# One program per engine, normalisations in pairs, gate stores from another queue, and prefetched rows in pieces in a two-stage encoder block

## The reference

```python
h = rms_norm(x, norm_mix); proj = h @ w_in           # q,k,v | B,C,u | two gates
att = stick_breaking_attention(q, k, v)              # 8 heads x 64, causal
y_a = att @ w_branch_a
y_b = (B * causal_conv3(C * u)) @ w_branch_b
x = x + (sigmoid(ga) * y_a + sigmoid(gb) * y_b) @ w_out
hx = rms_norm(x, norm_ffn)                           # second normalisation
q = (hx @ w_q).reshape(n, 8, 2, 128)
s = einsum('nhpc,hpkc->nhpk', q, sub_keys)           # 16 lists of 128 scores
# top 16 of each list, top 16 of the 16x16 sums -> 8*16 experts per token
w = softmax(best) * gelu(u_sel . hx)                 # u_sel, v_sel: rows of 16384x1024 tables
x = x + sum(w * v_sel)
out = rms_norm(x, final_norm)
```

## Time and profile before

| | |
|---|---|
| median of 3 runs | 1786.6 us (1784.12 to 1790.11) |
| the profiled execution's own time | 1788.63 us |
| its span, first to last instruction | 1786.9 us |
| PE busy | 1718.5 us, 96% of the span |
| first program | 0 to about 526 us |
| steps of the second program | about 526 to 1254 us |
| sums | 1254 to 1776 us |

### The profile page before, as it was taken

How to read it: one execution, slowest core, us unless ns; L and a number is a source line. 1 busy time by engine, 2 the same in 40 slices (tenths; PEclk the granted TensorE clock), 3 DMA queues, 4 the chain that set the end, 5 groups by cost and what they waited for, 6 DMA issues and landing times.

```text
span 1786.9 us, 24919 instructions
## 1 busy us (share of the span) xinstructions
PE 1718.5 (96%) x9066; PEld 1528.6 (86%) x9066; DVE 1278.5 (72%) x1834; ACT 768.5 (43%) x1086; POOL 775.1 (43%) x486
## 2 busy tenths in 40 slices
PE   6999999998979999999999999997999999999997
PEld 4777778877869999999999999997888888888886
DVE  1555511114889899989999797976678777877786
ACT  5444433234213466656666465553332332233222
POOL 3323334332411366655666678884333233323330
PEclk9999999998989999999999999998999999999999
DMA  4222223322225667766776899889999999999982
GB/s 153 71 71 68 62 71 94 105 71 71 83 83 204 204 239 245 243 234 240 244 244 224 317 341 345 289 309 340 345 395 350 351 364 347 349 358 358 347 328 104
DMA packets 211428, 413.79 MB, mean 232 GB/s; under 512 B 11408, under 2 KB 150704, under 8 KB 205744
## 3 DMA queue, kind: packets, MB, share of 16 engines
q1 hardware_dynamic: 154352, 228.63, 37.6%
q0 software_dynamic: 36864, 134.23, 20.8%
q10 hardware_dynamic: 20160, 50.34, 7.5%
HBM read 360.73 MB, written 52.43 MB: 231 GB/s over the span
## 4 chain that ended last, share of the span: by engine, by line
PE 51%; DVE 7%; POOL 7%; DMA 2%; ACT 2%; issue 2%; ACTq 0%; DVEq 0%; POOLq 0%
PE psum L1133 27%; PE psum L1073 19%; POOL ring L1274 4%; PE psum L1063 3%; POOL grid L1293 2%; DVE ring L1391 2%; DMA expert_gate<-grid 2%; DVE ul L1316 1%; PE psum L1100 1%; POOL hot L1284 1%; DMA ring<-in_expert_u,index 1%; DVE hot L1379 1%; DVE acc L1396 1%; DVE hot L1381 1%; ACT hot L1190 0%
## 5 line engine op out<-in xcount | busy, mean ns | idle before, releaser
L1073 PE MATMUL psum<-xTh,uh 128*128 128x384 f32 x1024 | 356.9, 349 | 17.5 <-DVE ul L1316 17.1
L1073 PE MATMUL psum<-xTl,uh 128*128 128x384 f32 x1024 | 346.0, 338 | 0.0
L1073 PE MATMUL psum<-xTh,ul 128*128 128x384 f32 x1024 | 345.8, 338 | 0.0
L1274 POOL DMA_INDIRECT ring<-in_expert_v,index x128 | 177.8, 1389 | 349.5 <-DVE acc L1396 307.2
L218 POOL TENSOR_TENSOR wl<-raw,wh 128x1024 fp32r<-128x1024 f32 x72 | 172.4, 2401 | 329.5 <-ACT wh L490 329.5
L1133 PE MATMUL psum<-vh,dwl 128*128 128x512 f32 x768 | 298.8, 389 | 0.0
L1133 PE MATMUL psum<-vl,dwh 128*128 128x512 f32 x768 | 298.8, 389 | 0.0
L1133 PE MATMUL psum<-vh,dwh 128*128 128x512 f32 x768 | 298.8, 389 | 0.0
L1210 ACT ACTIVATE vh<-v_raw 128x4096 fp32r<-128x4096 f32 x32 | 116.2, 3632 | 338.8 <-PE psum L1133 304.7
L1274 POOL DMA_INDIRECT ring<-in_expert_u,index x128 | 179.6, 1403 | 130.1 <-DVE index L1341 59.0
L1391 DVE SCALAR_TENSOR_TENSOR ring<-ring,x 128x1024 f32<-128x1024 f32 x128 | 206.4, 1625 | 26.3 <-DMA ring<-in_expert_u,index 24.9
(11 more groups left out here) (189 smaller groups left out, 2800.8 us busy)
## 6 DMA issues: line engine op xcount, KB each, us to landing
u_raw<-in_expert_u SPq DMA_DIRECT2D x128, 512.0 KB
v_raw<-in_expert_v SPq DMA_DIRECT2D x32, 2048.0 KB, 12.0
expert_act<-hb ACTq DMA_DIRECT2D x128, 192.0 KB
expert_gate<-grid ACTq DMA_DIRECT2D x12, 2048.0 KB
dh<-expert_act SPq DMA_DIRECT2D x32, 768.0 KB, 4.4
dg<-expert_gate SPq DMA_DIRECT2D x32, 768.0 KB
raw<-in_w_in SPq DMA_DIRECT2D x40, 512.0 KB, 3.8
raw<-in_w_q SPq DMA_DIRECT2D x16, 512.0 KB, 3.9
```

What stands on the lines that cost most here:

```text
L1073: last = nc.tensor.matmul(zb[s][:, 0:DT], w[s][:, c, :], x[:, c, 0:DT], start=(c == 0 and i == 0), stop=(c == C - 1 and i == 2))
L1274: nc.gpsimd.indirect_dma_start(out=ring[k][:], out_offset=None, in_=tables[x // SLOTS], in_offset=bass.IndirectOffsetOnAxis(ap=index[:, x ...
```

## The change

It does five things. (1) The two programs become functions for each engine, called one after the other inside one `nc.Block()`; the wait between them is gone, PE transposes the rows of step 0 before the last projection, and PSUM banks of the steps are swapped for that. ACT instead of DVE copies the score lists, and DVE does squares of the second normalisation; DVE leaves parts 4 to 11 of head 6 to the second program's steps 0 to 2 (9, 6 and 5 parts there, where 4, 4 and 4 stood). (2) The first normalisation's scales are made in pairs of blocks; scaled rows are written in column halves; each `norm_project` multiplies with `wh` first and with `wl` in a second pass. (3) The four small parameter loads are issued by ACT, and the weight loads start when the third block of x is there. (4) SP issues the twelve stores of `grid`, between its loads of buffers 1 and 2. (5) The first two groups of expert_v are loaded in eight pieces of 512 KB, one for each of the rounds 22 to 29, and the loads of `dh` no longer wait for the last store.

The diff, without indentation changes and cut to its core:

```diff
-    with nc.Block() as block:
-        @block.sync
-        def _(sp_):
+    def mix_sync(sp_):
...
-            sp_.wait_ge(S["rows_in"], 64)
+            sp_.wait_ge(S["consts"], 1)
+        sp_.wait_ge(x_in[2], 16)
...
+        def norm_project(first, r, parts):
+            ring = len(nb_ring)
+            for ready, more, blocks in parts[:-1]:
+                pe.wait_ge(S["xn_ready"], ready)
+                if more:
+                    pe.wait_ge(S["xn_more"], more)
+                for c in range(ring):
+                    norm_transposes(c, blocks)
+            pe.wait_ge(w_hi[0], r + 1)
+            pe.wait_ge(taken[0], r)
+            for c in range(C):
+                for n, x in enumerate((xh, xl)):
+                    pe.wait_ge(S[("xT_hi", "xT_lo")[n]], first + c + 1)
+                    nc.tensor.matmul(pj[0][:], wh[0][:, c, :], x[:, c, :], start=(c == 0 and n == 0), stop=False)
...
+                if c + ring < C:
+                    norm_transposes(c + ring, blocks)
+            pe.wait_ge(w_lo[0], r + 1 + PRIMED)
+            for c in range(C):
+                last = nc.tensor.matmul(pj[0][:], wl[0][:, c, :], xh[:, c, :], start=False, stop=(c == C - 1))
...
-            norm_project(0, NB, 0)
+        norm_project(0, 0, ((2, 0, (0, 1)), (3, 1, (2, 3)), (5, 1, range(NB))))
...
-            norm_project(C, 2 * NB, L5)
+        norm_project(C, L5, ((7, 3, range(NB)), (11, 3, range(NB))))
...
+        pe.wait_ge(u_in[0], 16)
+        for c in range(C):
+            last = nc.tensor.transpose(psum[6 + c // 4][:, c % 4 * P:c % 4 * P + P], u_raw[0][:, c * P:(c + 1) * P], ident[:])
+        last.then_inc(ut_full[0], 1)
             project(1, L5 + LISTS // 2 - 1, xh, xl)
...
             high(0, 0)
+        norm_hi(0, 0)
             high(1, 0)
             nc.scalar.preload_act_table_set("natural_log_exp_and_others")
-            norm_hi(0, 0)
...
+            norm_hi(C, C)
+        high(1, L4 + C // 2)
...
+        def copy_list(i, slot):
+            act.wait_ge(S["s_full"], i * 2 + (slot + 1 + PRIMED))
+            nc.scalar.activation(score[:, :, at, :], zt[slot][:].rearrange("p (b o k) -> p b o k", b=NB, o=1), ACT.Copy).then_inc(S["s_out"], 1)
...
+        for h in range(HEADS - 1):
+            dve.wait_ge(S["s_out"], h * 2 + 2 + PRIMED)
+            for k in range(12 if h < HEADS - 2 else AHEAD):      # AHEAD = 4
+                rank(dve, h, k)
...
+        def send(q):
+            sp_.wait_ge(S["g_sum"], 8 * q + 8 + PRIMED)
+            sp_.dma_start(gd[:, :, :].rearrange("b p x -> p b x")[:, q:q + 1, :], grid[:].rearrange("p j n -> p (j n)").unsqueeze(1)).then_inc(S["g_out"], 16)
...
+        for r in range(1, STEPS // 4):
+            load(r, range(2))
+            if 4 * r - 4 in SEND:
+                send(SEND[4 * r - 4])
+            load(r, range(2, 4))
+            if V_EARLY <= r < V_EARLY + 2 * G4:                  # V_EARLY = 22
+                if r == V_EARLY:
+                    sp_.wait_ge(S["selT_full"], DB)
+                load_part(*divmod(r - V_EARLY, G4))
+        for s in range(2):
+            load_acts(s, slice(s, s + 1))
...
             high(0)
+        last_list()
             for n in range(STEPS):
                 if n + 1 < STEPS:
                     high(n + 1)
-                if n in SEND:
-                    send(SEND[n])
...
                 if n < 3:
-                    for k in range(4 * n, 4 * n + 4):
-                        rank(dve, HEADS - 1, k)
+                if n == 0:
+                    dve.wait_ge(scores_out, LISTS + PRIMED)
+                for k in range((AHEAD, 13, 19)[n], (13, 19, 24)[n]):
+                    rank(dve, HEADS - 2 + k // 12, k % 12)
```

More of the change, by code:

```diff
@@ L47 @@
 PRIMED = 1
+AHEAD = 4
 Q0, K0, V0 = 0, SBW, 2 * SBW
@@ L514, in pair @@
-            def pair(p, r, before=None):
-                high(2, r)
-                take(0, r, qT[:], scale=HD ** -0.5)
+            act.wait_ge(S["var_ready"], g + 1)
+            nc.scalar.activation(rs[:, 2 * g:2 * g + 2], var[:, 2 * g:2 * g + 2], ACT.Sqrt).then_inc(S["root_ready"], 1)
+        act.wait_ge(S["scales"], 2)
+        nc.scalar.activation(xn[:, NB - 1, 0:T], acc[:, NB - 1, 0:T], ACT.Copy, scale=rs[:, NB - 1:NB]).then_inc(S["xn_more"], 1)
+        high(0, 0)
+        norm_hi(0, 0)
@@ L517, in pair, with gated @@
+        pair(0, 0)
+        with act.Fori(1, PAIRS) as p:
+            pair(p, p * 2, before=p - 1)
+        R0 = PAIRS * 2
+        def gated(r, c, before=None):
+            both_highs(c)
+            if before is not None:
                 high(0, r + 1)
-                take(1, r, kT[:])
+                exps(before, 0)
                 high(1, r + 1)
-                if before is not None:
-                    exps(before, 0)
-                    exps(before, 1)
-                take(2, r, vT[:])
@@ new lines, in mix_scalar @@
+        take_keys(2)
+        take_keys(3)
+        nc.scalar.preload_act_table_set("sqrt_and_others")
+        act.wait_ge(S["oT_full"], C - 2 + PRIMED)
+        take(0, L4 + C // 2 - 1, ot[0][:])
+        high(0, L4 + C // 2)
+        take(1, L4 + C // 2 - 1, ot[1][:])
+        act.wait_ge(S["x_added"], C + PRIMED)
+        for b in range(NB // 2, NB):
+            nc.scalar.activation(squared[:, b, D - 2 * P:D], acc[:, b, D - 2 * P:D], ACT.Square,
+                                 accum_out=ss[:, 1, b:b + 1]).then_inc(S["sq_done"], 1)
@@ new lines, in mix_scalar, with take_query @@
+        act.wait_ge(S["var_ready"], 3)
+        nc.scalar.activation(rs, var, ACT.Sqrt).then_inc(S["root_ready"], 1)
+        act.wait_ge(S["scales"], 3)
+        for b in range(NB // 2, NB):
+            nc.scalar.activation(xn[:, b, 0:T], acc[:, b, 0:T], ACT.Copy, scale=rs[:, b:b + 1]).then_inc(S["xn_more"], 1)
+        norm_hi(C, C)
+        high(1, L4 + C // 2)
+        def take_query(i, slot):
+            act.wait_ge(S["s_full"], i * 2 + PRIMED)
+            take(slot, i + (L4 + C // 2), ot[slot][:])
```

1839 lines of the change are left out of this document (923 added, 916 removed).

## The result

The changed kernel takes 1768.3 us in the median (1768.17 to 1768.36, 4 runs), the kernel before beside it 1785.4 us (1783.02 to 1790.11, 4 runs). The ratio is 0.9897, 95% interval 0.9883 to 0.9911: faster, by some 17 us or 1%. The profiled execution took 1768.36 us, with a span of 1766.6 us; before the span was 1786.9, so the traces differ by 20.3 us and the medians by 17. The profiled execution of the kernel before took 3 us more than its median here, so what follows place by place adds up to 3 us more than the medians show.

The account below looks back on a forecast made before the run. PE, busy 96%, was taken to bound the kernel, so its gains before 1254 us should reach the end. Terms 4.6 + 1.5 + 7.8 + 4.3 + 4.4 = 22.6 us gave 1764.0 against the median; 8-in-10 range 1753 to 1778.

Parts of the forecast that it names:

- Start: First normalisation: ACT's new order and half blocks let the second projection begin at about 25.2 instead of 29.85; gain 4.6 us.
- Second normalisation: Around 400 us: DVE's early squares and half-width rows start the transposes sooner; gain 1.5 us, bounds 0 and 3.
- Boundary: Between the two programs: first products 13.7 us earlier, partly lost to DVE's ranking and the clock; gain 7.8 us, bounds 4 and 13.
- The charge of 1.2 us for the clock: At the boundary: a 2.8 us idle of PE may lower the granted clock; half of a drop charged.
- Rival 1: DVE's ranking paces PE in steps 0 to 10, with two full clock drops; boundary gives 3.2, time 1768.6; chance 0.12.
- Pieces of expert_v: Near 1100 us: 512 KB pieces instead of 2 MB remove most of a 5.35 us stall; gain 4.3, bounds 0 and 5.35.
- Stores from SP: At the last grid store: two queues instead of three shorten the 12.75 us gather to about 8.5; gain 4.4, bounds 0 and 7.3.
- Rival 2: Gathers wait for bytes, not turns, so neither pieces nor queue help; 8.7 us go, time 1772.7; chance 0.20.
- Rival 3: Everywhere: every gain comes at its upper bound, 34.7 us in all, time 1752; chance 0.08.
- Rival 4: Stores block SP's queue, delaying loads of buffers 2 and 3 behind each store; slower, 1800; chance 0.08.
- Rival 5: No change: POOL, on the chain of waits from 1053 to 1205, eats all but 2 us; chance 0.06.
- The signs: Expected: second projection about 25, no sequencer wait near 517; wrong if u_raw waits, 12 us gathers, or clock below 0.9 after 517.

Follow-up runs that it names:

- k: Changed kernel with ACT's order at the start as before the change, both high parts and the table load ahead of the first xTh: 1773.2 us, ratio 0.9922.
- j: Changed kernel with PE waiting for all four blocks' rows before transposing the first chunk, scales still made in pairs: 1770.2 us, ratio 0.9901.
- a6: Changed kernel with AHEAD at 6 instead of 4, so DVE ranks two more parts before splitting the first chunks: 1766.0 us, ratio 0.9881.
- h: Changed kernel with the eight expert_v pieces issued two to a round over rounds 22 to 25, before 1060 us: 1768.5 us, ratio 0.9893.
- u2: Changed kernel with the first expert_v rows in two loads of 2 MB instead of eight of 512 KB: 1767.9 us, ratio 0.9894.
- c: Changed kernel with AHEAD at 6, DVE's second expert_v part behind step 127's low part, and gates 0 ahead of activations 1: 1764.5 us, ratio 0.9864.
- d: Changed kernel with c's gate order and second-part placement, h's pieces, AHEAD at 8, DVE's other parts 6, 5, 5: 1762.5 us, ratio 0.9860.
- u1: Changed kernel with the twelve grid stores issued by ACT again, at the same steps as before: 1775.7 us, ratio 0.9926.
- b3: Changed kernel with grid stores of 256 KB instead of 2 MB, plus 84 further 256 KB stores giving the bytes back: 1758.9 us, ratio 0.9835.

## Why the prediction was right, and where it was not

The time came out 4.3 us above the 1764.0 forecast, within the range. Start and boundary were sized well. Of the two terms on transfers, one was too large by 3.3 us, and the other came near its sum at a place that I had ruled out, which is luck.

**Start, 4.6 predicted, 5.15 measured.** The place and the mechanism hold: the second projection at 24.70 where I had 25.2, held at last by POOL's `wl` as I had written. k shows that ACT's order makes 2.7 of the 5.15, and j that PE's start on the first pair adds nothing, which the prediction had left mixed. The other 2.4 us (half rows, the low pass behind, earlier weight loads) were not taken apart.

**Second normalisation, 1.5 predicted, 2.6 measured.** The transposes begin 2.4 us earlier than before, counted from the start's gain, where I had 2.3. The last wait is POOL's low part, as I had it, but 11.8 us behind the first transpose instead of my 12.7: that is the error. PE was at the lower clock only up to 404.0, 4.1 us behind the first transpose; before, a window that ends 5.5 us behind it (407 to 413) still has 0.50. Whether that made the 0.9 us was not tested, and no experiment took this term apart.

**Boundary, 7.8 predicted, 8.1 measured.** The waits of 2.8 and 1.55 us that I had counted out are in the trace as 2.79 and 1.37, and a6 shows by its edit that DVE's parts make the first. The products of step 3 began at 529.52; with the 7.75 us won before, 8.7 us were left of the boundary there, where I had 9.6, and the first products were already 0.3 us later than my chain. Steps 3 to 7 took back 0.6 us, as I had it. The charge of 1.2 us for the clock was not paid here, and so the two errors nearly cancel. It was not wrong to fear a drop: the same idle of 2.79 us stands in ten kernels with this boundary, and in two of them, h and j, the clock did fall. But it was priced wrongly: steps 1 to 8 take 41.2 us in h and 40.6 in j, against 40.7, because PE then waits less for DVE. Rival 1 charged 5.8 us for two full drops and falls with that; that its 1768.6 is almost the measured time is chance.

**Pieces of expert_v, 4.3 predicted, 1.0 measured; this is the step that failed.** "The stall costs 3.7 + 1.65": right for the kernel before, and u2 shows the same mechanism once more, with 4.47 us of DVE's wait. The 1.0 us is itself within the scatter, so nothing was gained. What I missed is that the grid store which comes every eight steps is also 2 MB at once. Before, the store of 1112 us came right behind that stall, when DVE and POOL had just got ahead of a PE that stood still, and it cost PE nothing. With the first stall gone, the store is the one that strikes: in h with 5.36 us and no piece near, in the changed kernel with a wait of PE of 1.9 us behind it and two of 0.4. (The changed kernel has another wait of 1.3 us at 1086.82, ahead of the store, behind a row on which DVE spent 4.50 us; a6, c, d, h and j do not have it.) I had priced the removal of one burst against a trace in which its neighbour was free only because of it. That the store was free because of the slack is read from the traces: in before and in u2 PE has no wait behind it, in the others with 2 MB stores it has. With the stores small too, the pieces deliver: 71.9 us for steps 100 to 113, against 76.9. That a large load of expert_v beside small stores would bring the stall back was not tried.

**Stores from SP, 4.4 predicted; undoing the move alone costs about 5 us (u1), but at another place.** I had written that "ACT's own stall behind POOL and behind its 192 KB store is at other steps covered", and that a fairer share for the gather at the last store would bring it. Both are wrong. Steps 42 to 44 and 78 to 80, where the softmax's two table loads stand behind the store in ACT's stream, were not covered. Their removal is 2.9 us, in the traces before and after and in u1 alike; smaller losses make it 3.6 and 4.8 for all steps up to 100. At the last store nothing came. The gathers issued beside it took longer, not less:

```profile
ring<-in_expert_u,index POOLq DMA_INDIRECT x5, 14.0
```

These are the five of 1185.3 to 1193 in the changed kernel, with 14.0 us from issue to landing in the median, where I had "about 8.5". PE's single wait of 4.9 us is gone there, but one of 2.24 us at 1181.90 and three of 0.35 to 1.1 us up to 1212 stand in its place, and the time from step 121 to the sums is 0.2 us longer. The wait at 1181.90 lies ahead of the last store. Its chain goes back through the gather of 1171.59, which took an ordinary 6.14 us, and through POOL to the landing of the store of 1139.81: here POOL was late, not the transfer. I had written that POOL's wait for a landed store "should not grow"; it grew from 11.7 to 29.0 us, for the most part in place of waits for ACT. The gain in the end had to wait for the gates, which took 23.16 us to land at 1.03 of the DMA engines' share; before they were 3.2 us late for DVE, now 4.9. The Trainium skill (DMA: Bandwidth & Descriptors, Issuing engines are not separate DMA queues) says that transfers interleave on the same 16 DMA engines whoever starts them, and that several issuers save only issue time, which is small. The traces agree for the transfers: the gather beside the last store took 12.75 us with ACT as issuer, and the median of five was 14.0 with SP. The saving of u1 is not issue time, but what ACT did not have to wait for ahead of its issue.

**The rivals.** Rival 2 (transfers stay slow, bytes and not turns, 1772.7) was half right: its 8.7 us stayed away for those two places as it said, by 7.9, and its own sign came, gathers of 12 us and more at the last store. But b3 shows that the cause up to step 113 is not the bytes. Of the 7.9 us, 3.6 came in at the steps up to 100, which nobody had, and 2.0 in the other three places. Its support was also misread: 357 GB/s was not "as much as anywhere", since the page of the kernel before has slices of 395 and 364 GB/s. Rival 3 (1752) lies 16 us below the result. Rival 4 (the store blocks SP's queue) is not seen: PE never waited for `u_raw`. Rival 5 (POOL takes back all but 2 us) falls with the 20.3 us. POOL does hold PE at one place, 1181.90, as told above.

**The signs.** The second projection at 24.70, no wait for the sequencer and 2.79 us in step 1 came as written; the wait in step 2 was 1.37, not 2 to 3, and the second projection of the second normalisation was 7.7 us earlier, not 6. No wait over 2 us stood around step 103 in the changed kernel, but one of 3.7 to 4.0 stood a few steps later in a6, c, d, h and j. Two of the three signs of a wrong prediction also came: the gathers kept 12 us, and the granted clock was 0.89 over 1220 to 1250, where it had been 0.84 before. The number was right although the part on the transfers was not.

The sum of the places was 20.3 in the trace against 22.6: the hit is in part luck, an error of -3.3 (pieces) and one of about -1 (stores) being partly made up by +0.55, +1.1 and +0.3 at start, normalisation and boundary. At its own place the term for the stores was off by 4.6.

## What to carry to other kernels

Before pricing the removal of one large transfer, list all transfers of its size in the stretch: one may be free only because the stall of the other gave it slack, and then the loss moves and stays. When a gather is late, look at how the transfers beside it are cut and not only at their bytes: stores of 256 KB in rows of 2 KB carried more GB/s past the gathers than 2 MB in rows of 16 KB, without a wait up to step 113 (whether the size or the rows did it is open). And a store belongs on an engine for which waiting costs nothing: what it costs is everything behind the wait in that engine's stream, to be looked for where that engine has its rarest and longest work, not at the average step.

## What the runs showed of the hardware

The Trainium skill (DMA: Bandwidth & Descriptors, Measured) advises pieces of 1 MB or more to reach most of the bandwidth. By that rule b3, with its stores of 256 KB, should move its bytes more slowly than the changed kernel. It moved 342 GB/s at a DMA share of 0.97, against 316 at 0.89, over 1060 to 1130, beside loads of 512 KB and row gathers. That is 353 and 355 GB/s for a full share, an estimate from these rows: the small stores cost no rate that shows here. (The page's table is of loads into SBUF issued from GpSimd; the pieces here are stores from SP, and b3 also had more bytes to move, so this is no clean test of it.)

The same idle of PE does not always have the same effect on the granted clock. Ten kernels have the wait of 2.79 us at the boundary, behind 80 us (420 to 500) in which PE had been busy all the time. In eight of them the window of 500 to 530 has 1.00; in h and in j it has less:

```profile
500.00:530.00 30.00, 27.21 (x151) 25.71 (x151) 27.45 (x123) 9.25 (x12) 0.00 (x0) 0.89 0.31 101
...
500.00:530.00 30.00, 27.21 (x160) 25.57 (x159) 27.49 (x123) 9.43 (x13) 0.00 (x0) 0.94 0.31 101
```

At the end of the steps, after an idle of 4.77 us, the changed kernel's window of 1220 to 1250 had 0.89.

The gates, 768 KB a load, took 23.16 us to land beside another such load, two of 768 KB for the activations and the row gathers, two and a half times as long as the store of 2 MB ahead of them (9.1 us).
